# Prompt attention: values stationary, four heads' turned probabilities moved together, and the gate turned instead of the output

## What is computed

```python
def _sparse_attend(q, k_sel, v_sel, valid):     # per position: its own selected keys
    logits = einsum('btgrd,btkgd->btgrk', q, k_sel)
    logits = where(valid, logits, -inf)
    p = softmax(logits, axis=-1)
    o = einsum('btgrk,btkgd->btgrd', p, v_sel)

y = x + (o * silu(gate)) @ w_out
```

## Time and profile before

| | us |
|---|---|
| median of 3 runs | 1838.19 |
| lowest, highest | 1835.1, 1839.62 |
| span of the profiled execution | 1776.7 |
| the profiled execution's own time | not given with it; it lies among runs of 1835.1 to 1839.62, so about 61.5 us lie around the span |
| TensorE, VectorE, ScalarE, GpSimd busy | 1689.8, 1262.0, 764.5, 533.1 |
| `prompt_attend`, first logits to last residual | 535.5 to 833.3 |

### The profile page before, as it was taken

One profiled execution on the slowest core, in us unless ns is written; L12 is line 12 of the kernel. 1 busy time (PEld: TensorE's weight loads), 2 busy tenths in 40 slices (PEclk: granted clock), 3 DMA queues, 4 the chain that ended last, 5 costly groups with the idle time before them and its releaser, 6 DMA issues. The chain is left out here.

```text
span 1776.7 us, 26877 instructions
## 1 busy us (share of the span) xinstructions
PE 1689.8 (95%) x10109; PEld 967.8 (54%) x10109; DVE 1262.0 (71%) x2081; ACT 764.5 (43%) x1812; POOL 533.1 (30%) x632
## 2 busy tenths in 40 slices
PE   8999999999998999998999999999998879999999
PEld 6534434444446566665444544444435866777775
DVE  2399969999996798992696554646454677777773
ACT  2357867874225343333211242232212656554551
POOL 2502200100112111000225777777722512222320
PEclk9999999999999999999999999999998869999999
DMA  7406440110026111202413455555689444434321
GB/s 231 136 1 220 160 146 15 40 49 30 30 79 253 65 48 58 98 24 80 127 44 101 128 172 172 168 171 166 198 283 338 126 150 102 130 100 109 94 58 59
DMA packets 164024, 211.35 MB, mean 119 GB/s; under 512 B 45576, under 2 KB 114720, under 8 KB 163872
## 3 DMA queue, kind: packets, MB, share of 16 engines
q1 hardware_dynamic: 121912, 153.62, 26.6%
q0 software_dynamic: 16896, 50.35, 9.2%
q10 hardware_dynamic: 25088, 5.66, 1.5%
HBM read 165.86 MB, written 43.74 MB: 118 GB/s over the span
## 5 line engine op out<-in xcount | busy, mean ns | idle before, releaser
L1578 POOL DMA_INDIRECT scores<-in_cache_k,rowidx x128 | 135.6, 1059 | 39.5 <-issue 36.7
L2211 POOL DMA_INDIRECT home<-in_cache_v,rowidx x128 | 132.9, 1038 | 39.0 <-issue 38.4
L1189 DVE MAX8 top_v<-scores 128x8 f32<-128x4100 f32 x32 | 141.6, 4427 | 0.4
L1191 DVE FIND_INDEX8 top_i<-top_v,scores 128x8 uint32<-128x4100 f32 x32 | 141.5, 4422 | 0.0
L1193 DVE MATCH_REPLACE8 scores<-top_v,scores 128x4100 f32<-128x4100 f32 x32 | 141.2, 4413 | 0.0
L186 ACT ACTIVATE junk_topk_h<-key_mask,bs_cand 128x640 f32<-128x640 f32 (+1 forms) x104 | 102.0, 983 | 32.0 <-DVE bs_cand L196 25.8
L1399 PE MATMUL ring<-w_out_att,ogT_blk 128*128 128x512 f32 x256 | 113.0, 600 | 1.0 <-ACT ogT_blk L1432 0.9
L965 PE MATMUL acc<-w_out_att,xnT 128*128 128x512 f32 x256 | 112.7, 593 | 0.0
L965 PE MATMUL acc<-w_kvq,xnT 128*128 128x512 f32 x256 | 111.4, 593 | 0.0
L3600 PE MATMUL PY<-home,ogT_dn 128*128 128x512 f32 x224 | 101.8, 596 | 0.0
L1432 ACT COPY pT_blk<-tp_blk 128x512 f32<-128x512 f32 (+3 forms) x96 | 43.2, 486 | 121.4 <-PE tp_blk L1369 121.2
(11 more groups left out here) (560 smaller groups left out, 3598.4 us busy)
## 6 DMA issues: line engine op xcount, KB each, us to landing
S_s<-in_dn_w_in SPq DMA_DIRECT2D x24, 512.0 KB, 4.8
qkv_d<-y_ch SPq DMA_DIRECT2D x24, 512.0 KB, 3.7
qkv_t<-qkv_d SPq DMA_DIRECT2D x8, 1536.0 KB, 8.0
home<-in_dn_w_in SPq DMA_DIRECT2D x5, 2048.0 KB, 13.9
x<-in_x_all SPq DMA_DIRECT2D x8, 512.0 KB, 3.5
w_kvq<-in_att_w_in SPq DMA_DIRECT2D x2, 2048.0 KB, 13.0
qT_d<-qTb SPq DMA_DIRECT2D x8, 512.0 KB, 2.7
gate_d<-sgate SPq DMA_DIRECT2D x8, 512.0 KB, 3.1
```

Of the source, the lines that this page charges most:

```text
L1189: link(dve.max(v, scores[:]))
L1191: dve.max_index(top_i[:, 8 * r:8 * r + 8], v, scores[:])
L1578: pool.indirect_dma_start(rows[:, j % KR, c, :], None, ck, bass.IndirectOffsetOnAxis(ap=idx[:, c, query(j):query(j) + 1], axis=0)).then_in ...
L2211: pool.indirect_dma_start(vg[:, j % VR, c, :], None, cv, bass.IndirectOffsetOnAxis(ap=rowidx[:, c, query(j):query(j) + 1], axis=0)).then_i ...
```

## The change

`weigh` takes a group k of four heads at once: the values' tile is stationary and the turned probabilities of the four heads, 512 columns, move past it. The result is the output already turned (head dimension on partitions, 4 heads x 128 positions along the free dimension). So the output is no longer turned; instead the gate is, after GpSimd has multiplied it by the inverse row sums (`gated` now works on the gate alone, one instruction, and the last half on VectorE). VectorE multiplies the turned output, straight out of PSUM, by the turned gate (`gated_out`) into `ogT_blk`. `take_out`, `turn_out` and `normed` go. `pT_blk` holds two groups of four heads and moves to the space of `xnT`. The group's `weigh` comes at steps hc = 4, 8, 12, ..., the gate's turn at steps 6, 10, 14, ..., and at the end the last group is split in three heads and one.

```diff
--- before.py
...
-    OG_AT, Y_AT, RES_AT = 3, 4, 5
+    Y_AT, RES_AT = 4, 5
+    NG, LAST = NB * G, NB * G - 1
...
-        pT = sb("pT_blk", [P, 2, NB, P])
+        pT = keep["xnT"][:].rearrange("p k n -> p (k n)")[:, 0:2 * NB * GRP * P].rearrange("p (u k h q) -> p u k h q", u=2, k=NB, h=GRP)
+        gT = sb("gT_blk", [P, H, P])
         ogT = sb("ogT_blk", [P, H, P])
...
+            if s >= 6 and s % 4 == 2:
+                turns.append(("g", (s - 6) // 4))
...
+        turns.append(("g", LAST))
...
+                    sp.wait_ge(tp_done, turned(("g", 2 * i + 1)))
...
             def gated(k):
                 i, u = divmod(k, 2)
-                hh = slice(4 * u, 4 * u + 4)
-                v = og[:, i % 2, 512 * u:512 * (u + 1)]
+                v = gate[:, i % 2, 512 * u:512 * (u + 1)].rearrange("p (h e) -> p h e", e=HD)
                 if u == 0:
                     pool.wait_ge(g_in[i % 2], 16 * (i // 2 + 1))
-                pool.wait_ge(o_taken, 4 * k + 4)
-                link(pool.tensor_tensor(v, v, gate[:, i % 2, 512 * u:512 * (u + 1)], ALU.mult))
                 pool.wait_ge(ri_ok, k + 1)
-                v = v.rearrange("p (h e) -> p h e", e=HD)
-                pool.tensor_tensor(v, v, ri[:, hh].unsqueeze(2).broadcast_to([P, 4, HD]), ALU.mult).then_inc(og_ok, 1)
+                pool.tensor_tensor(v, v, ri[:, 4 * u:4 * u + 4].unsqueeze(2).broadcast_to([P, 4, HD]), ALU.mult).then_inc(gr_ok, 1)
 
...
-            def weigh(hc):
-                g = hc % H // GRP
-                pe.wait_ge(tp_evac, turned(("p", hc)))
-                if hc >= 2:
-                    pe.wait_ge(o_taken, hc - 1)
-                for k in range(tiles(hc)):
-                    ins = pe.matmul(ops[:, hc % 2, 0:HD], pT[:, hc % 2, k, :], v_nat[:, k + 1, g * HD:(g + 1) * HD],
-                                    start=(k == 0), stop=(k == tiles(hc) - 1))
+            def weigh(k, bank, first, last):
+                i, g = divmod(k, G)
+                pe.wait_ge(tp_evac, turned(("p", 4 * k + last - 1)))
+                if bank >= 2:
+                    pe.wait_ge(og_ok, bank - 1)
+                for j in range(i + 1):
+                    ins = pe.matmul(ops[:, bank % 2, first * P:last * P], v_nat[:, j + 1, g * HD:(g + 1) * HD],
+                                    pT[:, k % 2, j, first:last, :].rearrange("p h q -> p (h q)"), start=(j == 0), stop=(j == i))
                 ins.then_inc(o_done, 1)
 
-            def turn_out(i):
-                pe.wait_ge(og_ok, min(2 * (i + 1), LAST_HALF))
-                if i == NB - 1:
-                    pe.wait_ge(og_last, 4)
-                turn(("og", i), og[:, i % 2, :], H)
+            def turn_gate(k):
+                i, u = divmod(k, 2)
+                if k == LAST:
+                    pe.wait_ge(gr_last, 1)
+                else:
+                    pe.wait_ge(gr_ok, k + 1)
+                turn(("g", k), gate[:, i % 2, 512 * u:512 * (u + 1)], GRP)
 
             def out_proj(i):
                 dst = claim(("y", i))
-                pe.wait_ge(tp_evac, turned(("og", i)))
                 if i == 0:
                     pe.wait_ge(once, 32)
                 for a in range(0, DM, 512):
                     for h in range(H):
+                        if a == 0 and h % GRP == 0:
+                            pe.wait_ge(og_ok, 2 * i + h // GRP + 1)
+                        if a == 0 and h == H - 1 and i == NB - 1:
+                            pe.wait_ge(og_ok, NG + 1)
                         ins = pe.matmul(dst[:, a:a + 512], ogT[:, h, :], wo[:, h, a:a + 512], start=(h == 0), stop=(h == H - 1))
                 ins.then_inc(ring_done, 1)
 
@@ -1405,15 +1407,16 @@
                 i, h = divmod(hc, H)
                 if hc + 2 < NH:
                     logits(hc + 2)
-                if i >= 1 and h == OG_AT:
-                    turn_out(i - 1)
+                if hc >= 6 and hc % 4 == 2:
+                    turn_gate((hc - 6) // 4)
                 if i >= 1 and h == Y_AT:
                     out_proj(i - 1)
                 turn_probs(hc)
-                if hc >= 1:
-                    weigh(hc - 1)
-            weigh(NH - 1)
-            turn_out(NB - 1)
+                if hc >= 4 and hc % 4 == 0:
+                    weigh(hc // 4 - 1, hc // 4 - 1, 0, GRP)
+            weigh(LAST, LAST, 0, GRP - 1)
+            turn_gate(LAST)
+            weigh(LAST, NG, GRP - 1, GRP)
             out_proj(NB - 1)
 
...
-            def take_out(hc):
-                i, h = divmod(hc, H)
-                act.wait_ge(o_done, hc + 1)
-                if i >= 2 and h == 0:
-                    act.wait_ge(tp_done, turned(("og", i - 2)))
-                act.copy(og[:, i % 2, h * HD:(h + 1) * HD], ops[:, hc % 2, 0:HD]).then_inc(o_taken, 1)
+                    act.copy(dst[:, n:n + m, :], tpb[:, b % 2, 0:m, :]).then_inc(tp_evac, 1)
+
+            def probs_turned(hc):
+                k = hc // GRP
+                if k >= 2 and hc % GRP == 0:
+                    act.wait_ge(o_done, k - 1)
+                evac(("p", hc), tiles(hc), pT[:, k % 2, :, hc % GRP, :])
+
+            def gate_turned(k):
+                u = k % 2
+                if k >= 2:
+                    act.wait_ge(og_ok, k - 1)
+                evac(("g", k), GRP, gT[:, 4 * u:4 * u + 4, :])
 
...
+                if hc >= 6 and hc % 4 == 2:
+                    gate_turned((hc - 6) // 4)
...
+                probs_turned(hc)
+            gate_turned(LAST)
 
...
             def inverse(k):
-                u = k % 2
+                i, u = divmod(k, 2)
                 dve.wait_ge(exp_ok, 4 * k + 4)
                 if k >= 2:
-                    dve.wait_ge(og_ok, k - 1)
-                dve.reciprocal(ri[:, 4 * u:4 * u + 4], rs[:, 4 * u:4 * u + 4]).then_inc(ri_ok, 1)
-
-            def normed(hc):
-                i, h = divmod(hc, H)
-                if hc == 4 * LAST_HALF:
-                    dve.wait_ge(og_ok, LAST_HALF - 1)
-                    dve.wait_ge(g_in[i % 2], 16 * (i // 2 + 1))
-                dve.wait_ge(exp_ok, hc + 1)
-                link(dve.reciprocal(ri[:, h:h + 1], rs[:, h:h + 1]))
-                dve.wait_ge(o_taken, hc + 1)
-                dve.scalar_tensor_tensor(og[:, i % 2, h * HD:(h + 1) * HD], og[:, i % 2, h * HD:(h + 1) * HD], ri[:, h:h + 1],
-                                         gate[:, i % 2, h * HD:(h + 1) * HD], ALU.mult, ALU.mult).then_inc(og_last, 1)
+                    dve.wait_ge(gr_ok, k - 1)
+                ins = dve.reciprocal(ri[:, 4 * u:4 * u + 4], rs[:, 4 * u:4 * u + 4])
+                if k < LAST:
+                    ins.then_inc(ri_ok, 1)
+                    return
+                link(ins)
+                dve.wait_ge(g_in[i % 2], 16 * (i // 2 + 1))
+                v = gate[:, i % 2, 512 * u:512 * (u + 1)].rearrange("p (h e) -> p h e", e=HD)
+                dve.tensor_tensor(v, v, ri[:, 4 * u:4 * u + 4].unsqueeze(2).broadcast_to([P, 4, HD]), ALU.mult).then_inc(gr_last, 1)
+
+            def gated_out(k, bank, first, last):
+                i, u = divmod(k, 2)
+                dve.wait_ge(tp_evac, turned(("g", k)))
+                dve.wait_ge(o_done, bank + 1)
+                if i >= 1:
+                    dve.wait_ge(ring_done, at["y", i - 1] + 1)
+                h = slice(4 * u + first, 4 * u + last)
+                dve.tensor_tensor(ogT[:, h, :], ops[:, bank % 2, first * P:last * P].rearrange("p (h q) -> p h q", q=P), gT[:, h, :], ALU.mult).then_inc(og_ok, 1)
 
...
+                if hc >= 4 and hc % 4 == 0:
+                    inverse(hc // 4 - 1)
+                if hc >= 7 and hc % 4 == 3:
+                    k = (hc - 7) // 4
+                    gated_out(k, k, 0, GRP)
                 if i == NORM_AT and h in (6, 7):
                     t = h - 6
                     dve.wait_ge(rs_ok, t + 1)
@@ -1528,8 +1531,9 @@
                     dve.scalar_tensor_tensor(nxt[:, t, :], nxt[:, t, :], rss[:, t, :], nxt[:, 2, :], ALU.mult, ALU.mult).then_inc(xn_ok, 1)
                 between(dve, NX_P + int((NX_B - NX_P) * ahead / total + 0.5), NX_P + int((NX_B - NX_P) * (ahead + span(hc)) / total + 0.5))
                 ahead += span(hc)
-            normed(NH - 2)
-            normed(NH - 1)
+            inverse(LAST)
+            gated_out(LAST, LAST, 0, GRP - 1)
+            gated_out(LAST, NG, GRP - 1, GRP)
             residual(NB - 1)
 
 
```

More of the change, by code:

```diff
@@ L1211, in sem @@
             return new_sem(nc, env, name)
-        q, gate, x, og = (keep["first_blk"][k] for k in ("q", "gate", "x", "og"))
+        q, gate, x = (keep["first_blk"][k] for k in ("q", "gate", "x"))
         lm = sb("lm", [P, LR, SEQ])
@@ L1239, in prompt_attend @@
         o_done = sem("ob_done")
[L1240 to L1241 removed]
+        gr_ok, gr_last, og_ok, ri_ok = sem("gr_ok"), sem("gr_last"), sem("og_ok"), sem("ri_ok")
         pch = sem("pool_chain_pa")
[L1243 removed]
         y_out = [env["stores"][f"y1_out{u}"] for u in range(2)]
@@ L1253, in prompt_attend @@
```

(43 more changed lines are left out.)

1 line of the change is left out of this document (removed).

## The result

The changed kernel takes 1859.6 us (median of 6 runs) against 1837.6 before; the ratio is 1.0139 [1.0111, 1.0166]. Forecast: 1839.6, range 1829 to 1848, "the same". It is slower, and beyond the range.

What follows compares the result with a forecast made beforehand. The prediction took `prompt_attend` as bound by TensorE early and by TensorE and VectorE late. Its terms, -2.3 -2.1 -4.3 +6.0 +4.1 = +1.4 us on 1838.19, gave 1839.6 us, "the same", range 1829 to 1848.

Steps and rivals of the forecast that it cites:

- Term 1: In `weigh`, values stationary turn 576 narrow passes into 144 of 512 columns: -2.3 us.
- Rival C: Weight loads set the pace of `weigh`'s narrow passes, so -48.7 us: 1791, or an estimated 1801; chance 0.03.
- Term 2: Turning the gate instead of the output removes TensorE's stalls behind `turn_out`, with some new copy waits: -2.1 us.
- Term 3: At the stage's end, `out_proj` follows the last `weigh` without a gap (-2.5) and at full clock (-1.8): -4.3 us.
- Term 4: At head 5, logits wait longer for the ring slot of VectorE's residual, by one head's `weigh`: +6.0 us.
- Term 5: VectorE's new `gated_out` lies on the path in late blocks, and `out_proj` waits for it: +4.1 us, bounds 0 and +8.
- the walk: Block 6 followed instruction by instruction on TensorE and VectorE: `out_proj` waits 0.1 and ends 1.35 us later than before.
- rival D: `gated_out` on VectorE costs 1.2 us, twice the price: +3.7, 1843 us; chance 0.50 together with the main case.
- rival A: TensorE's queue and the `lm` slots absorb the longer ring wait and `gated_out`: at most -8.7, 1829.5 us; chance 0.25.
- Rival B: TensorE's waits after the residual halve its clock in four of blocks 3 to 7: 1849 us; chance 0.19.
- Nothing outside the stage is changed.: Only `prompt_attend` is touched; later stages merely shift by what it gains or loses, so no time was counted there.

Runs made afterwards that it cites:

- before again: The kernel before, unchanged, profiled a second time: span 1829.0 us, `prompt_attend` 297.2 us, ratio 0.9994.
- experiment 6: The kernel before with 15 more VectorE instructions of 512 columns where `gated_out` stands after the change: ratio 1.0038.
- experiment 2: The changed kernel with the group's `weigh` split by tiles over three heads in a row: ratio 1.0079.
- experiment 5: The kernel before with the narrow `weigh` of four heads in one stretch, one copy out for the four, output still turned: ratio 1.0171.
- 11: The changed kernel with `weigh` spread over three steps, 79 padding waits on TensorE and a new table placing VectorE's search pieces: ratio 0.9995.
- 10: The changed kernel with `weigh` spread over three steps and 79 already fulfilled padding waits on TensorE: ratio 1.0032.
- experiment 7: The changed kernel with 247 already fulfilled wait instructions on TensorE behind the stage's last `out_proj`: 1882.5 us.
- experiment 8: The changed kernel with 871 already fulfilled wait instructions on TensorE behind the stage's last `out_proj`: 1943.1 us.
- 9: The changed kernel with 103 already fulfilled waits on TensorE, 17 or 18 ahead of each of six logits: ratio 1.0080.
- 12: The changed kernel with `weigh` spread over three steps and ScalarE copying the turned output instead of `gated_out`, gate left out: ratio 1.0043.
- 3: The changed kernel with VectorE's search pieces placed where TensorE has its lumps: ratio 1.0164.
- Experiment 4: The changed kernel with ScalarE copying the turned output instead of VectorE's `gated_out`, gate left out of the product: ratio 1.0084.

## Why the prediction was wrong

**Term 1 was right.** `weigh` has 160 passes, 128 of 512 columns at 0.43 (12 in 5.15, from 716.02 to 721.17), 16 of 384 and 16 of 128. Rival C falls with it. (Its 1791 and 1801 take term 1's 2.3 off twice; 1793 and 1804 follow from its own numbers.)

**Term 2 was about right.** The gate's copies are waited for 2.2 us in eight places, and the 2.6 for `ogT_blk` and 0.9 for GpSimd are gone: -1.3 in waits, forecast -2.1.

**Term 3 was right in its working, not in its size.** The end, TensorE's timeline after:

```profile
833.57 5.33 PE L1379 MATMUL o_blk<-xnT,v_nat 128*128 128x384 f32 x16
838.73 0.60 PE L1366 MATMUL tp_blk<-ident,w_kvq 128*128 128x128 f32 x4
839.17 1.95 PE L1379 MATMUL o_blk<-xnT,v_nat 128*128 128x128 f32 x16
840.96 13.90 PE L1401 MATMUL ring<-w_out_att,ogT_blk 128*128 128x512 f32 x32
```

`out_proj` follows the last `weigh` without a gap and lasts 13.90. But before again has 13.97 without any change, so the -1.8 for the clock was not the change's. Head 7 is asked for 14 passes (6.0 us) after the first, not 7, which only makes the step safer. From the last narrow pass to `out_proj` before again has 3.0 us, after has none but 0.44 for the gate's transposes: -2.5.

**Term 4 was about right**: the wait for the residual went from 5.5 to 10.2, +4.7, forecast +6.0.

**Term 5 and the walk are where it failed in the stage.** `gated_out` costs what I said (0.69, rival D falls), and in before's rhythm fifteen such instructions cost 2.4 together (experiment 6). What the term left out is one more user of the ring. I followed the slot that `logits(hc+2)` wants after the residual; `out_proj` wants a slot as well, that of `masked(8i+5)`, and the walk let TensorE reach `out_proj` at 735.3, 32.1 behind the end of the last one, without asking when that `masked` is done. Its own list had `masked(53)` start at 737.0; with a length of 1.15 it ends at 738.1, 2.8 behind 735.3, where the walk wrote a wait of 0.1. Up to there the walk agrees with the trace: the logits ahead of `out_proj` start at 745.91 and their passes take 1.5, which is 32.0 behind the end of the last `out_proj` at 715.37. `out_proj` then starts at 749.88, 34.5 behind. I had VectorE's instructions written out in order and didn't check that one consumer against them. The same wait is 2.20 in block 5, 2.31 in 6, 3.62 in 7.

With it goes a wrong picture: that with VectorE "never idle" the added work simply adds. The prediction named idle time of VectorE in blocks 5 to 7 as what would prove it wrong, and there are 8.1 and 5.3 us of it in block 6 and the one after (3.8 and 2.4 in before again). The sum as measured, in waits of TensorE against before again: term 5 has +8.1 (`out_proj` for `masked`), +1.5 (`logits` for `masked`), +4.5 (transposes for ScalarE's exponentials and copies of probabilities), and +1.8 for a slow `out_proj`, below: 15.9 for a forecast of 4.1. The 4.5 stand in a place that the prediction put at nothing, because ScalarE and GpSimd "idle beside the others"; experiment 2 has 0.2 left of them, so they belong to the lump too. Terms 1 to 4 give -2.3 -1.3 -2.5 +4.7 = -1.4. Together +14.5 of the 16.5; 2.0 I can't assign.

That the lump is the cause is shown from both sides: alone in before it costs 15.9 by the seventh `out_proj` (experiment 5), and after gets 9.7 back when the same passes are spread (2); the places of the search, which fit the old rhythm, give back another 5.3 (11 against 10), 1.8 of which is the slow `out_proj` of 10. With both, the stage is at 298.6, 1.4 from before. So rival A, that the lumps are absorbed, was wrong by the price of the lump itself.

**Rival B came in a part, and in how large a part is chance.** The windows view of after at the slow `out_proj` (the clock is the third number from the end):

```profile
699.80:702.00 2.20, 2.17 (x4) 1.00 (x5) 2.20 (x6) 1.03 (x2) 0.45 (x1) 0.68 0.00 0
702.00:704.00 2.00, 2.00 (x4) 0.84 (x3) 2.00 (x1) 0.00 (x0) 0.59 (x1) 0.50 0.00 0
704.00:706.00 2.00, 2.00 (x6) 0.84 (x5) 1.97 (x2) 0.00 (x0) 0.00 (x0) 1.00 0.00 0
```

After the wait of 2.20 the granted clock is 0.50 (1.2 GHz) from 700.6 to 704.0, and `out_proj` takes 15.70 for 13.90 before: +1.8 once. The waits of 2.31 and 3.62 brought no such fall in this execution. In other executions of the same stage, with the same three waits, it came elsewhere. In experiment 7 only the last was followed by it:

```profile
802.00 15.70 PE L1401 MATMUL ring<-w_out_att,ogT_blk 128*128 128x512 f32 x32 [3.62 <-DVE nmx_blk L1479]
```

In experiment 8 all three were: 15.70, 15.70 and 16.95, 6.65 us over 13.90, close to what rival B gave for four places. So the length of one wait doesn't decide it. The Trainium skill (TensorE: Matmul & The Clock Gate, how oscillation bites in real kernels) says that a matmul engine which idles for long enough between bursts runs the next one at the half rate. The half rate after a wait agrees with the traces in kind, but not every one of these waits brought it. Most of the loss was the waiting itself.

**The second failed step is a sentence: "Nothing outside the stage is changed."** True of the code, not of the time: +9.5. Counting TensorE's instructions in the traces (loads, passes and waits) up to the first matmul of `acc_s`, and setting beside them what the last stages took:

| executions | instructions | fewer than before | last stages, us |
|---|---|---|---|
| before, before again, 6 | 11054 | 0 | 442.7, 441.2, 442.9 |
| 8 | 11055 | 0, but for 1 | 441.3 |
| 9, 10, 11 | 10286 | 3 x 256 | 440.1, 443.0, 440.0 |
| 5 | 11006 | 48 | 452.2 |
| 2, 12 | 10207 | 3 x 256 + 79 | 446.9, 450.0 |
| after, 3, 4 | 10183 | 3 x 256 + 103 | 450.7, 456.1, 448.1 |
| 7 | 10431 | 2 x 256 + 111 | 453.6 |

The seven executions at before's place in units of 256 instructions take 440.0 to 443.0, the seven at other places 446.9 to 456.1, whatever else the kernels do. Experiment 5 shows that it isn't the number that is missing: 48 do it. The stalls themselves say the same. In the two rows of `join16` 87 loads over all 14 traces come after a standstill put down to "issue". Counted in the same way from the start of the program, 79 of them have number 194 or 195 in a run of 256, whatever the length of the stream; the number of the other 8 moves with the code. At before's place that number falls mostly into the first row of `join16`, at the others always into the second.

The page counts the transfers of instructions; before and after have (packets, MB, share):

```profile
q8 instruction: 81, 1.33, 0.3%
```

```profile
q8 instruction: 78, 1.28, 0.3%
```

The count follows the length of TensorE's stream (79 in experiment 7, 81 in 8), at 16.4 KB each. The period of 256 instructions is shown by the traces. That 256 instructions are one such transfer, and that the stall is the engine waiting for its next one, is inferred: no record shows what it waited for. The Trainium skill (Runtime: NRT & Kernel Launch, Instruction fetch mechanics) says that an engine's instructions come in blocks of 16 KiB, 256 of them, and that crossing into the next is mostly hidden. The size agrees with the 16.4 KB and the number with the period; "mostly hidden" doesn't hold here, if the inference is right, in a stretch of 32-wide matmuls that follow one another fast.

Had both been in the sum, it would have read 1.4 + 11.8 (term 5) + 9.5, about 23; the medians differ by 22.0, and the ratio says 25.5 [20.4, 30.5].

The two parts are shown each by its own experiments; that they add up to the whole so closely is partly luck, since the stage scatters by 4.5 us between executions of the same code (313.7 to 318.2) and the last stages by 8 (448.1 to 456.1).

**What stays open.** Experiment 4's timed ratio is 10 us below after's, and so is its profiled span, 1847.6 for 1857.8; but only 4.6 of that lie in the stage and the last stages, and 5.6 in stretches that don't differ in code. Why the last stages lose more with the stall in the second row of `join16` than with it in the first isn't shown, nor which wait brings the half rate.

## What to carry to other kernels

A reorder that keeps the work but makes one engine's bursts longer has to be checked against every consumer of the slots behind it, by the time at which the slowest feeder is done; mean busy shares say nothing when two engines are both near full and take turns. Where a schedule of filler work (here the search pieces) was fitted to one rhythm, price the new rhythm with the filler in its old places, and refit it before judging the idea. And where a profile compares two kernels of different instruction counts, look at the untouched stages too: pad the shorter one back by the missing count, modulo 256, before crediting the difference to the change.

## What the runs showed of the hardware that I had not expected

The time of untouched code, 441 us long, moves by about 10 us (440.0 to 443.0 against 446.9 to 456.1) with the position of TensorE's instructions modulo 256. A wait that is already fulfilled costs TensorE 0.109 us: 247 of them start within 26.8 us, 871 within 94.5. And whether a wait of TensorE is followed by half the clock changes from execution to execution: after the same three waits of 2.20, 2.31 and 3.62 us it was the first alone, the last alone, or all three.
